# Second feed-forward block of a two-block transformer kernel: opening, turns between stages, five slabs held for the last columns, and GpSimd for the low parts of the reloaded gated blocks

## What is computed

```
h = rmsnorm(x, pre_ffn_w[l])
f = (jax.nn.silu(h @ w_gate[l]) * (h @ w_up[l])) @ w_down[l]
x = x + rmsnorm(f, post_ffn_w[l])
```

## Time and profile before

| | |
|---|---|
| median of the runs | 2907.8 us |
| the profiled execution's own time | 2905.17 us |
| span of its instructions | 2902.9 us |
| PE (TensorE matmul) busy | 2820.1 us, 97% |
| VectorE (DVE) busy | 1563.9 us, 54% |
| ScalarE (ACT) busy | 1032.5 us, 36% |
| GpSimd (POOL) busy | 369.5 us, 13% |
| DMA, mean | 105 GB/s |
| FF2 from g1's second half to the end | about 2208 to 2902.9 us |

### The profile page before, as it was taken

How to read it: one execution, slowest core, us unless ns; L and a number is a source line. 1 busy time by engine, 2 the same in 40 slices (tenths; PEclk the granted TensorE clock), 3 DMA queues, 4 the chain that set the end, 5 groups by cost and what they waited for, 6 DMA issues and landing times.

```text
span 2902.9 us, 31767 instructions
## 1 busy us (share of the span) xinstructions
PE 2820.1 (97%) x12895; PEld 2286.5 (79%) x12895; DVE 1563.9 (54%) x1948; ACT 1032.5 (36%) x1396; POOL 369.5 (13%) x326
## 2 busy tenths in 40 slices
PE   9999999999999999999999999999999999999987
PEld 7877668888888888788878888666787788887876
DVE  7776544453545454543324444665647777764533
ACT  4313442331212121331235665655354322223422
POOL 1213112000000000111002222123421000000120
PEclk9999999999999999999999999999999999999998
DMA  3224523111111111144623322665641322225632
GB/s 118 88 73 141 151 61 111 51 40 55 46 53 41 58 35 61 56 148 151 218 80 100 99 78 77 196 199 150 222 160 59 102 80 87 87 86 172 199 116 95
DMA packets 105041, 304.62 MB, mean 105 GB/s; under 512 B 14392, under 2 KB 19128, under 8 KB 104896
## 3 DMA queue, kind: packets, MB, share of 16 engines
q1 hardware_dynamic: 90400, 256.22, 28.4%
q0 software_dynamic: 14496, 46.38, 4.6%
HBM read 238.42 MB, written 64.13 MB: 104 GB/s over the span
## 4 chain that ended last, share of the span: by engine, by line
PE 83%; DVE 8%; ACT 4%; issue 2%; DMA 2%; POOL 1%; SPq 0%; DVEq 0%; POOLq 0%; ACTq 0%
PE ps L225 82%; DVE cacc L196 2%; ACT PB L190 1%; PE ps L228 1%; POOL ga L193 1%; DVE PB L196 1%; DMA RBc<-scr_inv 1%; DVE AL L196 0%; DVE YA L193 0%; DVE dwt L193 0%; ACT gt L190 0%; ACT AH L190 0%; DVE stk L193 0%; DVE tr L196 0%; ACT stk L190 0%
## 5 line engine op out<-in xcount | busy, mean ns | idle before, releaser
L225 PE MATMUL ps<-AH,wh 128*128 128x512 f32 (+1 forms) x1608 | 644.7, 401 | 27.3 <-DVE wl L193 9.2
L225 PE MATMUL ps<-AH,wl 128*128 128x512 f32 (+1 forms) x1608 | 629.4, 391 | 0.0
L225 PE MATMUL ps<-AL,wh 128*128 128x512 f32 (+1 forms) x1608 | 629.0, 391 | 0.0
L193 DVE TENSOR_TENSOR wl<-raw,wh 128x1024 fp32r<-128x1024 f32 (+2 forms) x154 | 196.3, 1275 | 405.0 <-ACT wh L190 404.8
L225 PEld LDWEIGHTS ps<-AH,wh 128*128 128x128 f32 (+1 forms) x1608 | 302.1, 188 | 103.3 <-issue 18.8
L225 PEld LDWEIGHTS ps<-AH,wl 128*128 128x128 f32 (+1 forms) x1608 | 301.8, 188 | 66.8
L225 PEld LDWEIGHTS ps<-AL,wh 128*128 128x128 f32 (+1 forms) x1608 | 302.5, 188 | 64.3 <-issue 2.9
L190 ACT ACTIVATE wh<-raw 128x1024 fp32r<-128x1024 f32 (+4 forms) x201 | 188.1, 936 | 370.5 <-PE ps L225 367.8
L225 PE MATMUL ps<-stk,stk 128*128 128x512 f32 (+3 forms) x832 | 242.3, 405 | 12.2 <-DVE small L205 6.3
L225 PEld LDWEIGHTS ps<-stk,stk 128*128 128x128 f32 x832 | 146.6, 190 | 80.7 <-issue 32.4
L225 PE MATMUL ps<-UH,wh 128*128 128x512 f32 x528 | 205.5, 389 | 0.0
(11 more groups left out here) (267 smaller groups left out, 4701.1 us busy)
## 6 DMA issues: line engine op xcount, KB each, us to landing
raw<-in_w_up SPq DMA_DIRECT2D x44, 512.0 KB, 3.3
dwr<-in_dn SPq DMA_DIRECT2D x88, 256.0 KB, 2.9
swr<-in_w_gu SPq DMA_DIRECT2D x38, 512.0 KB, 3.7
raw<-in_w_w2in SPq DMA_DIRECT2D x32, 512.0 KB, 4.3
scr_u<-uu SPq DMA_DIRECT2D x22, 512.0 KB, 5.1
xin<-in_xT SPq DMA_DIRECT2D x16, 512.0 KB, 8.7
stk<-scr_ka SPq DMA_DIRECT2D x32, 256.0 KB, 8.1
raw<-in_w_w2v SPq DMA_DIRECT2D x16, 512.0 KB, 3.3
```

Source lines behind the costliest of these rows:

```text
L193: return Issued(self, self.e.tensor_tensor(out, a, b, op))
L225: return Issued(self, self.e.matmul(out, l, r, start=start, stop=stop))
```

## The change

- `HELD` goes from 14 to 17: five slabs are held back instead of eight.
- Opening: on VectorE and ScalarE the sums, their high and their low parts are moved ahead; on SyncE spill(0) stands behind `gate_load(0)` and `up_load(0)` instead of ahead of them.
- Turn from the Strassen columns to down: `d_low(0)` to `d_low(6)` are spread between and behind the last column's additions instead of standing together ahead of `value`; `u_low` is made by GpSimd, in its order with `summed`; the first blocks are reloaded earlier, as far as their buffers are read out.
- Turns between the passes: `evacuate` and `square` are taken one at a time, five slabs later; `stats` at w = 53, sqrt and reciprocal at 61 instead of 60.
- ScalarE copies bank 6 to a new SBUF tile `RD`; `normed(n)` reads that, and TensorE's wait at w = 66 is for the copy (`nrb` 8) and no longer for the eight multiplications (`fmu` 8).
- ScalarE's four copies to `YD` stand behind all of its `d_high`.

```diff
-HELD = 14
+HELD = 17
...
+        self.RD = w.get("rd", [P, 512])
...
             if w == 66:
-                q.wait_ge(S.fmu, 8)
-            if w == 52:
+                q.wait_ge(S.nrb, 8)
+            if w == 53:
                 q.wait_ge(S.fe, 8)
                 q.wait_ge(S.aD, 7)
                 stats(8, 0, 4, 7)
...
-        for k in range(2):
+        for k in range(3):
             second(k)
         self.w_high(q, TILE["gu", ("u", 1)])
-        second(2)
         up(TILE["gu", ("u", 0)], 0)
+        sums_high(0)
+        second(3)
         self.norm_sqrt(q, 7, 4, 4)
+        sums_high(1)
         q.wait_ge(S.nrow, 7)
         q.act(self.RB[:, HALF[1]], self.bank(5), ACT.Copy).then_inc(S.nrb)
         up(TILE["gu", ("u", 0)], 1)
-        sums_high(0)
-        second(3)
+        self.w_high(q, TILE["gu", ("g", 2)])
         silu(0)
-        sums_high(1)
-        self.w_high(q, TILE["gu", ("g", 2)])
         sums_high(2)
+        sums_high(3)
         up_whole(1)
         silu(1)
         self.w_high(q, TILE["gu", ("u", 2)])
-        sums_high(3)
...
             for p in range(3):
-                if w == 22 * (p + 1) + 4:
-                    for n in range(4):
-                        square(p // 2, 4 * (p % 2) + n)
-            if w == 60:
+                if 0 <= w - 22 * (p + 1) - 8 < 4:
+                    square(p // 2, 4 * (p % 2) + w - 22 * (p + 1) - 8)
+            if w == 61:
                 self.norm_sqrt(q, 8, 4)
-            if w == 66 + HELD + 1:
-                for n in range(4):
...
+            if w == 66:
+                q.wait_ge(S.nrow, 8)
+                q.act(self.RD[:, :], self.bank(6), ACT.Copy).then_inc(S.nrb)
+        for n in range(4):
+            q.wait_ge(S.dn, 12 + n + 1)
+            q.wait_ge(S.fe, 12)
+            q.act(self.YD[:, 4 + n, HALF[1]], self.d_bank(3, n), ACT.Copy).then_inc(S.fe)
...
         for w in range(88):
             if w >= 7:
                 d_low(w)
-            if 4 <= w < 22:
-                u_low(w)
-            if 30 <= w < 52:
-                u_low(w - 8)
             for p in range(3):
-                if w == 22 * (p + 1) + 2:
-                    evacuate(p)
-            if w == 60:
+                if 0 <= w - 22 * (p + 1) - 7 < 4:
+                    evacuate(p, w - 22 * (p + 1) - 7)
+            if w == 61:
                 self.norm_recip(q, 8, self.last_col(0), 4)
             if 67 <= w < 71:
...
+                normed(2 * w - 134)
+                normed(2 * w - 133)
...
-        for n in range(1, 8):
+        for u in range(22):
+            u_low(u)
+        for n in range(1, 4):
+            summed(0, n)
+        for u in range(22, 44):
+            u_low(u)
+        for n in range(4, 8):
             summed(0, n)
...
             elif k < 4:
                 q.wait_ge(S.gem, GEM_END[TILE["gu", ("u", 2)]])
+            elif k < 16:
+                q.wait_ge(S.prd, 7 * (NQ - 1) + (1 if k < 8 else 2 if k % 2 == 0 else 5))
...
-        spill(0)
         q.wait_ge(S.tr3, 16)
...
         gate_load(0)
         up_load(0)
+        spill(0)
         spill(1)
...
                 for w in range(7):
                     d_load(w)
-                    if w < 4:
-                        u_load(w)
-                for u in range(4, 8):
-                    u_load(u)
+                    u_load(w)
+        u_load(7)
+        u_load(8)
         spill(PLAIN + NQ - 1)
+        u_load(9)
+        u_load(10)
```

More of the change, by code:

```diff
@@ L3285, in d_low @@
             q.tt(l, self.DWR[w % DW], f32(h), ALU.subtract).then_inc(S.dwl)
-        def u_low(u):
-            h, l = self.DU[u % 22]
-            q.wait_ge(S.duh, u + 1)
-            q.tt(l, self.DUR[u % 22], f32(h), ALU.subtract).then_inc(S.dul)
+        sums(0)
         self.w_low(q, TILE["gu", ("u", 1)])
         gate_half(0)
+        sums(1)
         self.norm_recip(q, 7, self.rc8[:, 4:8], 4)
+        sums(2)
         gate_half(1)
-        sums(0)
-        sums(1)
+        sums_low(0)
+        self.w_low(q, TILE["gu", ("g", 2)])
+        sums(3)
+        sums_low(1)
         gated(0)
-        self.w_low(q, TILE["gu", ("g", 2)])
-        sums_low(0)
-        sums_low(1)
-        sums(2)
+        sums_low(2)
         gate_whole(1)
         gated(1)
+        sums_low(3)
         self.w_low(q, TILE["gu", ("u", 2)])
-        sums_low(2)
-        sums(3)
-        sums_low(3)
         s_sums(0)
@@ L3361, in dve_ff2 @@
                 s_lows(n + 1, 0)
+            else:
+                d_low(0)
             shared_end(n)
@@ L3364, in dve_ff2 @@
                 s_lows(n + 1, 1, 2)
+            else:
+                d_low(1)
             gate_end(n)
@@ L3368, in dve_ff2, with evacuate, normed @@
             else:
-                for w in range(7):
-                    d_low(w)
-                    if w < 4:
-                        u_low(w)
+                d_low(2)
             value(n)
+        d_low(3)
         value_end(NQ - 1)
-        def evacuate(p):
+        for w in range(4, 7):
+            d_low(w)
+        def evacuate(p, n):
             c = HALF[p // 2]
-            for n in range(4):
-                q.wait_ge(S.dn, 4 * p + n + 1)
-                q.tt(self.YD[:, 4 * (p % 2) + n, c], self.d_bank(p, n), self.RB[:, c], ALU.mult).then_inc(S.fe)
+            q.wait_ge(S.dn, 4 * p + n + 1)
+            q.tt(self.YD[:, 4 * (p % 2) + n, c], self.d_bank(p, n), self.RB[:, c], ALU.mult).then_inc(S.fe)
+        def normed(n):
+            c = HALF[0]
+            q.wait_ge(S.nrb, 8)
+            q.wait_ge(S.sD, 8)
+            q.stt(self.YD[:, n, c], self.YD[:, n, c], self.V("postff", n), self.RD[:, :], ALU.mult, ALU.mult).then_inc(S.fmu)
         for w in range(88):
@@ L3456, in pool_ff2, with u_low @@
         S = self.S
+        def u_low(u):
+            h, l = self.DU[u % 22]
+            q.wait_ge(S.duh, u + 1)
+            q.tt(l, self.DUR[u % 22], f32(h), ALU.subtract).then_inc(S.dul)
         def summed(t, n):
@@ L3559, in sp_ff2 @@
             d_load(w)
-            if w < 21:
+            if 10 <= w < 21:
                 u_load(w + 1)
```

10 lines of the change are left out of this document (removed).

## The result

The changed kernel takes **2873.09 us** (median of 4 runs, 2870.92 to 2878.98), against 2908.34 (2907.36 to 2909.48) for the kernel before beside it: a ratio of 0.9882, with an interval of 0.9865 to 0.9899. Its profiled execution is the slowest of the four: 2878.98 us of its own time, span 2877.1. So the time needs two readings: FF2, which the change touches, and the identical code ahead of it.

The account below looks back on a forecast made before the run. TensorE, 97% busy, loses 35.6 us in five stretches of waiting and slow pace behind. Terms sum to -34.2: profiled 2905.2 becomes 2871.0; with the median 2.6 higher, forecast 2873.6 us, range 2869.5 to 2882.

Parts of the forecast that it names:

- g2's wait: Opening, ahead of g2: making its low part earlier on VectorE removes TensorE's wait and slow stretch, minus 6.8 us.
- The new wait at u2: Opening: u2's low part now hangs on spill(0)'s landing behind two loads, so TensorE waits there, plus 1.2 us.
- the opening only half works: Rival: spill(0) lands behind two full loads, u2's `wl` 3 us or more late, clock falls; 2877 us, chance 0.12.
- The first Strassen product: Opening: subtractions and first `swl` take some 4 us while u2 has 10.9, so TensorE's second wait goes, minus 5.9 us.
- Turn to down: Strassen columns to down: one low part, not eleven, ahead of `value`; bank 0 free 1.3 us early, minus 5.0 us.
- `value_end` doesn't take turns: Turn to down: with one input in PSUM, `value_end` isn't held up by GpSimd, leaving the turn its whole 1.3 us.
- The last pass: Ahead of the last pass: TensorE waits only for ScalarE's early copy of bank 6, not eight multiplications, minus 10.7 us.
- The held slabs: Before the end: 17 slabs whole and copies last remove the wait, minus 7.2 us; fewer 256-column matmuls, minus 0.5.
- The tail: Program's end: shorter matmul groups make VectorE about 0.5 us late, one GpSimd collision adds a little; plus 0.7 us.
- The 44 low parts: Low parts of reloaded blocks, moved to GpSimd: cost nothing on the path while each is ahead of its slab.
- each `d_low` may take 1.8 us in the first pass: First pass: always taking turns with GpSimd adds 1.1 us, giving 1.8 us of a slab's 2.72, which still fits.

Follow-up runs that it names:

- the first eight experiments: Changed kernel with, in turn: bank-6 copy undone, evacuations together, both, lows on VectorE, seven lows together, HELD 14, copies' old place, GpSimd's lows doubled; 2874.77 to 2885.90 us.

## Why the prediction was right

Forecast 2873.6, measured 2873.09; the range was 2869.5 to 2882.0. The agreement of the medians is closer than the noise ahead of FF2 deserves; the sum over FF2 is the better test, -34.2 against -33.7.

- **g2's wait, -6.8:** gone, the stretch is full, and g2's low part was ready at the very time that the forecast had.
- **The new wait at u2, +1.2:** 1.74. The forecast put spill(0)'s landing at 3.7 us behind its issue; it was 4.2, and the chain behind it was as listed (6.65 us for 6.6). So this one term was mis-sized, by half a us. The gap is the only long one left, as said, and the clock held in the changed kernel's profile. The rival "the opening only half works" was near: the nine profiles of kernels with this opening (the changed one, and the first eight experiments in the order above) have gaps of 1.74, 2.66, 1.87, 1.81, 2.31, 2.17, 2.59, 2.17 and 2.38 us. Behind 2.59 and 2.38 the clock fell for 3.4 us, behind 2.66 it did not.
- **The first Strassen product, -5.9:** gone. The first four `swl` are made from 2249.22 to 2253.3, and u2's 48 matmuls last until 2257.5. No run puts the opening's old order back, so that the new order took away this wait and g2's is read from the trace of the changed kernel alone; of the opening only the spill's place and the last `tl` were tested.
- **Turn to down, -5.0:** gone, by the order alone; the margin was as thin as stated, 1.15 us where the forecast had 1.3, and the run with the seven lows together shows it used up. That `value_end` doesn't take turns was right.
- **The last pass, -10.7:** gone, and worth nearly that (10.2 with both measures undone). The prediction credited the copy. The runs show the later, spread evacuations would have done it without the copy.
- **The held slabs, -7.2 and -0.5:** right in size. The prediction named both causes and did not divide them: 5.1 for the place of the copies, 1.7 for the number with its smaller matmuls and its tail.
- **The tail, +0.7:** 0.67, by shares other than forecast: VectorE was later by 0.26 us and not by a full half, and one meeting with GpSimd made the rest.
- **The 44 low parts, 0:** right, but so would leaving them on VectorE have been. That each `d_low` may take 1.8 us in the first pass was taken from the earlier trace rows, and it is what happens to those that meet one of GpSimd's (three in a row took 1.77 or 1.78 us from 2631.79 on; 66 of the 88 took 0.7), within the slab's 2.72. The Trainium skill's advice (GPSIMD Engine Reference, "Engine selection") to keep such work on VectorE isn't contradicted: GpSimd takes 1.29 us where VectorE takes 0.69, and nothing is won by moving.

The sum, with the two terms that were measured directly in place: -6.8 +1.74 -5.9 -5.0 -10.7 -7.2 -0.5 +0.67 = -33.7 us, the measured difference. The other six are prices from the rows of the kernel before, and the sum shows them right together.

## What to carry to other kernels

Price a wait by the whole stretch around it, the slow matmuls behind it included, and undo the remedies of a change in pairs as well as singly: two that cover the same wait each look worthless alone. Moving work to an engine that takes turns with the first gives little where the two work at once; first try the order of the first engine's list, where an instruction that blocks (a copy that waits for TensorE, a low part nobody needs yet) stands ahead of one that TensorE is about to ask for. At the end of a program look at when each engine's last instruction ends, not only at the last store.
